# Value products of an expert layer with the table as the moving operand, and ten halves of gathered rows moved between stages

## The reference

```
q = (xb @ w_q).reshape(T, 8, 2, 128)                 # 8 heads, two halves
sc = einsum('thcd,hckd->thck', q, sub_keys)          # 128 keys per half
...                                                  # top 16 of 16x16 sums per head: idx, best
g = softmax(best)
act = gelu(einsum('td,thkd->thk', xb, u_tab[idx]))   # u_tab: 16384 x 2048
out = einsum('thkd,thk->td', v_tab[idx], g * act)    # v_tab: 16384 x 2048
x = x + out;  y = rmsnorm(x, final_norm_g)
```

## Time and profile before

| | |
|---|---|
| Median of three runs | 1714.14 us (1712.58 to 1718.35) |
| The profiled execution | 1717.41 us |
| Its span | 1715.6 us |
| TensorE busy with products | 1689.2 us, 98% |
| VectorE busy | 1455.6 us, 85% |
| ScalarE busy | 982.2 us, 57% |
| GpSimd busy | 475.9 us, 28% |
| Moved by DMA | 495.08 MB, mean 289 GB/s |
| Granted clock of TensorE | 0.997 of full speed, 2.4 GHz |

### The profile page before, as it was taken

The page is one execution under the profiler, slowest core; times in us unless marked ns, Lnnn a source line. Parts: engine busy times, 40 slices in busy tenths (PEclk is TensorE's granted clock), DMA queues, the critical chain, the costliest instruction groups (busy, mean ns, idle before and its releaser), DMA issues. The chain is left out here.

```text
span 1715.6 us, 28790 instructions
## 1 busy us (share of the span) xinstructions
PE 1689.2 (98%) x10886; PEld 1600.7 (93%) x10886; DVE 1455.6 (85%) x2068; ACT 982.2 (57%) x1589; POOL 475.9 (28%) x331
## 2 busy tenths in 40 slices
PE   8999999999999999999999999999999999999997
PEld 7887778878999999999999999999999999999997
DVE  4545777568799998999999999779999989999996
ACT  5555565453465557777766555555555555555554
POOL 0002310015320001111113354114454535444451
PEclk9999999999999999999999999999999999999999
DMA  6765455676677878888888999999999999999994
GB/s 230 217 185 169 148 159 159 192 253 198 195 232 230 268 234 295 284 274 281 269 278 306 399 399 403 310 271 393 381 390 384 377 327 362 383 390 384 376 378 180
DMA packets 135735, 495.08 MB, mean 289 GB/s; under 512 B 15424, under 2 KB 15456, under 8 KB 135088
## 3 DMA queue, kind: packets, MB, share of 16 engines
q1 hardware_dynamic: 95760, 347.65, 59.3%
q0 software_dynamic: 39552, 145.07, 23.2%
q10 hardware_dynamic: 288, 0.55, 0.1%
HBM read 487.86 MB, written 5.34 MB: 287 GB/s over the span
## 5 line engine op out<-in xcount | busy, mean ns | idle before, releaser
L750 ACT ACTIVATE HI<-V_RAW 128x1024 fp32r<-128x1024 f32 x256 | 271.9, 1062 | 258.0 <-PE PS L1711 123.3
L1671 PE MATMUL PS<-xT,HI 128*128 128x384 f32 x2048 | 414.1, 343 | 2.0 <-ACT HI L750 1.1
L1711 PE MATMUL PS<-W,HI 128*128 128x384 f32 x2048 | 411.0, 340 | 1.1 <-DVE OUTA L1330 0.6
L1671 PEld LDWEIGHTS PS<-xT,HI 128*128 128x128 f32 x2048 | 347.4, 188 | 9.8 <-ACT HI L750 7.5
L1711 PEld LDWEIGHTS PS<-W,HI 128*128 128x128 f32 x2048 | 347.8, 189 | 3.3 <-DVE OUTA L1330 1.9
L1219 DVE TENSOR_TENSOR V_LO<-V_RAW,HI 128x2048 fp32r<-128x2048 f32 x128 | 293.2, 2290 | 44.5 <-ACT HI L750 44.5
L750 ACT ACTIVATE HI<-RING_RAW 128x1024 fp32r<-128x1024 f32 x256 | 269.9, 1054 | 101.4 <-DMA RING_RAW<-u_t 95.6
L1226 DVE TENSOR_TENSOR RING_LO<-RING_RAW,HI 128x1024 fp32r<-128x1024 f32 x249 | 294.9, 1221 | 5.2 <-ACT HI L750 5.1
L526 POOL DMA_INDIRECT PICKED<-peer_u,PK x128 | 160.9, 1257 | 497.9 <-DVE DOTS L1278 420.6
L526 POOL DMA_INDIRECT PICKED<-peer_v,PK x128 | 212.3, 1659 | 242.7 <-DVE ACC L1283 217.4
L1716 PEld LDWEIGHTS PS<-W,V_LO 128*128 128x128 f32 x2048 | 265.7, 191 | 0.0
(11 more groups left out here) (218 smaller groups left out, 1586.8 us busy)
## 6 DMA issues: line engine op xcount, KB each, us to landing
RING_RAW<-u_t SPq DMA_DIRECT2D x256, 512.0 KB, 5.0
V_RAW<-peer_v SPq DMA_DIRECT2D x256, 512.0 KB, 9.3
RAW<-w_in SPq DMA_DIRECT2D x80, 512.0 KB, 3.8
RAW<-w_out SPq DMA_DIRECT2D x32, 512.0 KB, 3.9
RAW<-wq_t SPq DMA_DIRECT2D x32, 512.0 KB, 4.7
x_spill<-X POOLq DMA_DIRECT2D x2, 1024.0 KB, 5.8
PICKED<-peer_u,PK POOLq DMA_INDIRECT x128, 8.1
PICKED<-peer_v,PK POOLq DMA_INDIRECT x128, 9.1
```

Source lines behind the costliest of these rows:

```text
L750: nc.scalar.activation(HI[:, n % HI_SLOTS, :], raw_of(n), ACT.Copy).then_inc(top_ready, 1)
L1671: return mm(PS[:, j % S_BANKS, 0:2 * ND].rearrange("p (a t) -> p a t", a=2), HI[:, n % HI_SLOTS, kk * P:(kk + 1) * P], xT[:, k, :, 0:ND], ...
L1711: return mm(PS[:, V_BANKS[i], 0:2 * ND].rearrange("p (a t) -> p a t", a=2), HI[:, v % HI_SLOTS, i * P:(i + 1) * P], weights_of(v), start=v ...
```

## The change

The value product is turned. The gated scores are now the stationary operand, 128 tokens at a time, and the table moves, 512 columns at a time. The 192 tokens' high and low parts, 384 columns of `W`, are laid out as three blocks of 128: tokens 0 to 127 high; tokens 128 to 191 high with their low beside; tokens 0 to 127 low. The results lie with tokens on partitions, in banks A (tokens 0 to 127) and B (tokens 128 to 191, high on partitions 0 to 63 and low on 64 to 127). There is one pass over the 128 steps, a step's two halves one after the other, so eight banks hold all 2048 columns. The ring has 12 slots. Weights are made once per four units (before, per two). At the end no transposes are needed: VectorE adds the banks to the residual, ScalarE copies the lower half of B over to `OTHER`, and GpSimd adds the gathered rows to the residual.

Of the gathered halves 92 stand in scoring, not 102: every fifth step of those from 36 to 86 has none. The value stage has 164, not 154, spread over units 14 to 241 with no gap in the middle.

```
-V_RING = 10
-V_PLACE = [8, 9, 4, 5, 6, 7, 0, 1, 2, 3]
+V_RING = 12
+V_PLACE = [10, 11, 6, 7, 8, 9, 2, 3, 4, 5, 0, 1]
...
-HALF_STEPS = sorted(list(range(SPREAD0 - 3, NKEYS - 7)) + list(range(SPREAD_END, NKEYS - 7, 2)))
-FREE_UNITS = [u for u in range(14, 250) if not NKEYS - 6 <= u < NKEYS + 2]
+HALF_STEPS = sorted([j for j in range(SPREAD0 - 3, SPREAD_END) if j % 5] + list(range(SPREAD_END, NKEYS - 7))
+                    + list(range(SPREAD_END, NKEYS - 7, 2)))
+FREE_UNITS = range(14, 242)
...
-V_BANKS = (5, 6, 7, 3, 4, 2, 0, 1)
+BANK_A, BANK_B = (5, 6, 4, 2), (7, 3, 0, 1)
...
         def weights_of(v):
-            return WHL[v // 2 % W_PAIRS][:, v % 2]
+            return WHL[v // 4 % W_PAIRS][:, v // 2 % 2]
...
+                if v == V_RING - 2:
+                    sp.wait_ge(summed, NKEYS)
...
-                    half, j = divmod(v, NKEYS)
+                    j, half = divmod(v, 2)
                     src = v_view[:, j, half * UNIT:(half + 1) * UNIT]
...  (GpSimd, after the last gather)
+            for half in range(2):
+                cols = slice(half * HALF, (half + 1) * HALF)
+                nc.gpsimd.tensor_tensor(X1R[NS:P, 1, cols], X1R[NS:P, 1, cols], ACC4[NS:P, cols], ALU.add)
+            for half in range(2):
+                cols = slice(half * HALF, (half + 1) * HALF)
+                nc.gpsimd.tensor_tensor(X1R[NS:P, 1, cols], X1R[NS:P, 1, cols], OTHER[NS:P, cols], ALU.add)
...  (VectorE, weights_lo)
+                for dst, first, end in ((ND, P, ND), (2 * ND - P, 0, P)):
+                    ins = v.tensor_tensor(pair[:, :, dst:dst + end - first], store[:, j:j + 2, first:end],
+                                          pair[:, :, first:end].bitcast(FP32), ALU.subtract)
...  (VectorE, add_out of 512 columns c)
+                v.tensor_tensor(X1R[0:NS, 1, cols], PS[0:NS, BANK_B[c], :], X1R[0:NS, 1, cols], ALU.add)
+                v.tensor_tensor(X1R[:, 0, cols], PS[:, BANK_A[c], :], X1R[:, 0, cols], ALU.add)
+                v.tensor_tensor(X1R[0:NS, 1, cols], OTHER[0:NS, cols], X1R[0:NS, 1, cols], ALU.add)
...  (TensorE)
-            def value_high(v, i):
-                return mm(PS[:, V_BANKS[i], 0:2 * ND].rearrange("p (a t) -> p a t", a=2),
-                          HI[:, v % HI_SLOTS, i * P:(i + 1) * P], weights_of(v),
-                          start=v % NKEYS == 0, stop=False)
-            def value_low(v, i):
-                return mm(PS[:, V_BANKS[i], 0:ND], low_of(N_U + v)[:, i * P:(i + 1) * P],
-                          weights_of(v)[:, 0, :], start=False, stop=v % NKEYS == NKEYS - 1)
+            def value_high(v, c):
+                cols, w, b = HI[:, v % HI_SLOTS, c * BANK:(c + 1) * BANK], weights_of(v), 2 * (v % 2) + c
+                mm(PS[:, BANK_B[b], :], w[:, P:2 * ND - P], cols, start=v < 2, stop=False)
+                mm(PS[:, BANK_A[b], :], w[:, 0:P], cols, start=v < 2, stop=False)
+                return mm(PS[:, BANK_A[b], :], w[:, 2 * ND - P:2 * ND], cols, start=False, stop=False)
+            def value_low(v, c, last=False):
+                cols, w, b = low_of(N_U + v)[:, c * BANK:(c + 1) * BANK], weights_of(v), 2 * (v % 2) + c
+                low_b = mm(PS[:, BANK_B[b], :], w[:, P:2 * ND - P], cols, start=False, stop=last)
+                low_a = mm(PS[:, BANK_A[b], :], w[:, 0:P], cols, start=False, stop=last)
+                return low_b, low_a
```

More of the change, by code:

```diff
@@ L862, in final_scale @@
                     .then_inc(act_scaled, 1)
+            low_out_of(0)
+            low_out_of(1)
             act.wait_ge(fg_ready, 16 * D // BANK)
-            final_squares(0, 0)
-            final_squares(0, 1)
-            root(8, SS[:, 6:7])
-            final_squares(1, 0)
-            for c, col in ((2, 3), (3, 10)):
-                act.wait_ge(out_added, 4 + c + 1)
-                squares(X1R[:, 1, c * BANK:(c + 1) * BANK], col, FJ[:, 0:BANK])
+            final_squares(0, slice(0, HALF), 3, 0)
+            low_out_of(2)
+            act.wait_ge(rows_in, 4)
+            final_squares(1, slice(0, HALF), 4, 1)
+            low_out_of(3)
+            for c, cols in ((2, slice(HALF, HALF + BANK)), (3, slice(HALF + BANK, D))):
+                for tt in range(TT):
+                    final_squares(tt, cols, 2 * c + tt + 1, (2 + tt) if c == 2 else (10 + tt))
+                    if c == 3 and tt == 0:
+                        root(8, SS[:, 6:7])
             final_scale(0, slice(0, BANK))
@@ L1324, in _ @@
                     weights_lo(0)
-            def flush(half, i, dst):
-                dve.wait_ge(half_done, DT * half + i + 1)
-                v.tensor_reduce(dst[:, i, 0:ND], PS[:, V_BANKS[i], 0:2 * ND].rearrange("p (a t) -> p t a", a=2), AX.X, ALU.add)\
-                    .then_inc(flushed, 1)
             for u in range(N_V):
+                if u % 4 == 2 and u + 6 < N_V:
+                    weights_lo(u // 4 + 2)
                 if u % 2 == 0:
-                    if u + 4 < N_V:
-                        weights_lo(u // 2 + 2)
-                    if u == NKEYS - 2:
-                        for i in range(DT):
-                            flush(0, i, OUTA)
                     low_pair(u + 4)
-                if u == 0:
-                    dve.wait_ge(ones, N_BATCH)
-                    v.tensor_reduce(SEL4[:], IDENT[:].rearrange("p (s t) -> p t s", t=NS), AX.X, ALU.add).then_inc(sel_ready, 1)
                 if u in HALF_UNITS:
@@ new lines, in value_lows, with value_done @@
+                ins.then_inc(low_used, 1)
+            def value_done(v, c):
+                low_b, low_a = value_low(v, c, True)
+                low_b.then_inc(b_done, 1)
+                low_a.then_inc(a_done, 1)
+            for v in range(N_V - 1):
+                pe.wait_ge(top_ready, N_U + v + 1)
+                if v % 4 == 0:
+                    pe.wait_ge(w_lo, v // 4 + 1)
+                for c in range(2):
+                    if v == 1:
+                        pe.wait_ge(summed, NKEYS - 1 + c)
+                    ins = value_high(v, c)
+                ins.then_inc(top_used, 1)
+                if v:
+                    value_lows(v - 1)
@@ L1781 @@
+            low_wait(N_U + N_V - 2)
+            for c in range(2):
+                value_done(N_V - 2, c)
+            pe.wait_ge(top_ready, N_U + N_V)
+            low_wait(N_U + N_V - 1)
+            for c in range(2):
+                value_high(N_V - 1, c)
+                value_done(N_V - 1, c)
 def kernel(**inputs):
```

175 lines of the change are left out of this document (68 added, 107 removed).

## The result

The changed kernel takes 1704.42 us (median of 4 runs, 1703.03 to 1705.69); the kernel before, beside it, 1715.28 (4 runs, 1712.58 to 1718.35). The ratio is 0.9936, 95% interval [0.9919, 0.9953]: about 11 us, 0.6% faster. 1697 was forecast, with 1687 to 1710 as the range.

The account below looks back on a forecast made before the run. TensorE was taken to bound the value stage and VectorE scoring with gates, DMA near full. 1717.41 - 8.5 - 10.2 + 2 - 1.0 = 1699.7 us against the profile, as a median 1697 us; range 1687 to 1710.

Parts of the forecast that it names:

- the term of scoring: Scoring with gates: ten halves fewer free VectorE, -8.5 us, bounds 0 and -9.5.
- that of the value stage: Value stage: 584.0 us instead of 594.2, -10.2 us, bounds -13.5 and -5; 2 us added for short stalls.
- The 0.24 us more per pair, 9.5 us in all, is VectorE: its own step is 5.78 us: Scoring: pairs with a spread take 5.72 us instead of 5.48 because VectorE's own work sets them.
- the price of another wait: Rival in scoring: the 0.24 us per pair is not VectorE's, so 8.5 us stay; 1705 us, chance 0.08.
- VectorE's step is as long as TensorE's: Scoring: the argument given against the rival that scoring gives nothing back.
- The value unit: Value stage: ten 512-column products at 0.228 us make 2.28 us per unit; the turn itself gains 0.01 us per unit.
- The columns-alone rival: Value stage: turned products reach 0.216 us, TensorE needs 553 us, then the queue decides; down to 1690 us, chance 0.05.
- DMA stalls: Value stage: 2 us added for short stalls, bounds 0 and +14.
- the lag of 9 us: Value stage: DMA needs 2.32 us per unit, lagging 0.04 us over 228 units; the ring's 13 us slack covers it.
- 395 GB/s: Value stage: the DMA rate that new units ask for, (1 + 0.719) loads per 2.28 us, against 383 before.
- The dearer-loads rival: Value stage: successive loads of two halves of the same rows cost more; at 10% more 1731 us, chance 0.09.
- The end: Last value product to last scaling: 9.8 us instead of 10.8, -1.0 us, bounds -3 and +3.

Follow-up runs that it names:

- moved92: Changed kernel with ScalarE's scaling of the one-hot tables moved to the next step, behind the copy `HOLES` and the first `top`: 1695.91 us, ratio 0.9891.
- before92: Kernel before, value products not turned, with 92 gathered halves in scoring and 164 in the value stage: 1714.36 us, ratio 0.9999.
- before_moved: Kernel before with only ScalarE's scaling of the one-hot tables moved later in its program, 102 halves in scoring: 1705.99 us, ratio 0.9948.
- t102: Changed kernel with turned value products but 102 halves in scoring, as in the kernel before: 1704.91 us, ratio 0.9941.
- nohalf_spread: Changed kernel with no half in the 48 steps with a spread, 54 in scoring and 202 in the value stage: 1733.0 us, one run.
- loadorder: Changed kernel with value loads in the order of before, all left halves then all right ones: 1703.08 us, ratio 0.9937.
- pool_late: Changed kernel with GpSimd's two multiplications by the final gain waiting for all of VectorE's additions: 1707.88 us, one run.

## Why the prediction came out as it did

The direction, the range and the likeliest stage were right. The time was 7 us too low, and that it was not further off is luck: the term of scoring was too good by 8 us, and that of the value stage too poor by 5.5.

**Scoring: wrong, and the step that failed is "The 0.24 us more per pair, 9.5 us in all, is VectorE: its own step is 5.78 us".** The step was as long as the pair because VectorE was carried along by it. Two numbers that I had read spoke against it. The 1.46 us from a half to the next instruction hold 0.23 us of idle, marked "issue", before `TMP`; an engine that sets the pace has none, and in moved92 the same instruction follows at once. In 236 us of scoring it was busy 222.97, 94%, so 13 us, 0.3 per pair, were free, more than the excess to be explained. The right case was among the rivals ("the price of another wait"), with 1705 us and a chance of 0.08; what I wrote against it, "VectorE's step is as long as TensorE's", holds for every engine in a ring and tells nothing. The measured price of the ring is 9.1 us (moved92 against the changed kernel's 272.14), so the size of the excess was right and its owner wrong.

**The value unit: mechanism right, size at the lower bound.** 2.267 us, 10 x 0.2267. A product with new weights each time stands as far from the next as those in the earlier trace rows. The stage is 580.48, not 584.0 us. From the kernel before, 256 x (2.293 - 2.267) is 6.7 us, the pass change 2.75 (9.63 less three units) and the last unit 4.6 (6.9 less 2.29): 14.0 against 13.7 measured. The pass change is dearer in that one profile than elsewhere: in before92 and before_moved the same three units take 7.75 and 7.78 us, and the stages are 592.13 and 592.14 us. So the usual gain of the stage is 11.7 us, of which 6.7 are the turned unit and 5 what it lets fall. I had put the turned unit at 0.01 us, "almost nothing"; it is 0.026, times 256. The columns-alone rival (0.216 us) is false. The section that the prediction names for it in the Trainium skill (TensorE: Matmul & The Clock Gate, section Back-to-back issue gap) gives that formula for an isolated product, and about 131 ns for products of 512 columns in a sustained stream. The trace agrees with neither: it shows 226.7 ns.

**DMA stalls: +2 forecast, none measured.** What was wrong is the lag of 9 us, worked out as work over share, with 1.43 us of engine time for a load and a share of 1.02 as the most. But that time isn't a fixed price: in the same window of 1170 to 1380 it is 1.34 us in the changed kernel (59.2% of 210 us for 48.60 MB), where it was 1.45 before, and in that window the rate was 382 GB/s at a share of 1.02 in before, and 389, 393 and 398 GB/s at 1.01 in t102, before92 and the changed kernel, about what each asked for. Only nohalf_spread, at 409 GB/s, made TensorE wait. The forecast's own "395 GB/s" was right as a demand and not a limit.

**The dearer-loads rival: false.** Loads of the two halves of the same rows cost 1.34 us of engine time from 1170 to 1380, those of loadorder, in the old order, 1.36 (60.5% of 210 us for 48.99 MB), and loadorder's time is the same. The pitch within a load is the same in all runs, so none tests what it costs.

**The end: -1.0 forecast, +1.7 measured.** I had 12 additions at 0.65 us, to +5.1 after the last product. They start at -2.8, and ten of them take 0.60 from start to start, but two wait for GpSimd, which the forecast left out, so they end at +6.4. Last scaling at 11.4 where 9.8 was forecast. Another 1.1 us lies behind it: 4.7 us from the last scaling to the end of the span before, 5.74 to 5.81 in every turned kernel. The stores (2.1 MB) begin when the first block is scaled and run on at about 390 GB/s. The first is issued at 1708.51, 2.4 us ahead of the end of the last scaling, in the kernel before, and at 1694.02, 1.9 us ahead, now, which is half of the difference; where the other half comes from is not tested.

The sum of the profiled differences, -0.5 - 1.4 - 13.7 + 1.7 = -13.9 us, was forecast as -17.7. The missed 8.0 us of scoring were made good in part by the stage, 5.5 us with the stalls.

Two sums of the prediction are slightly off, and neither moves its time: 14.6 us over 48 steps are 0.30 us each, not 0.29, and the bound of -13.5 us for the stage belongs to 0.2267 us per product; 0.227 gives -12.8.

## What to carry to other kernels

When an engine's step is as long as the period, look for idle time in it, however short and however it is labelled, before calling it the bound: without any, the engine sets the pace; with some, follow the releases around until they close, and look for an instruction in one engine's program that stands ahead of the one the ring needs. Here moving it cost nothing, and taking work off that stood beside the ring, 10 or 48 halves, gave nothing. Here a DMA share of 1.01 to 1.02 went with anything from 382 to 398 GB/s, so it didn't show that the engines could do no more; ask which engine waits for a load, and what the rate is when it does.

## What the runs showed of the hardware that was not expected

- **A neighbour on GpSimd lengthens some of VectorE's instructions.** A 64 x 512 addition with both inputs in SBUF takes 0.67 us, and 1.62 when it starts under one of GpSimd's multiplications; additions with one input in PSUM take 0.67 in the same microseconds (1688.09). In pool_late two SCALAR_TENSOR_TENSOR of 128 x 1 elements went from 0.16 to 1.80 and 2.26 us, while a TENSOR_SCALAR of that size kept its 0.15 (1691.83). The Trainium skill (SBUF — State Buffer, section SBUF: two separate sides) says that a VectorE instruction with two SBUF inputs and a GpSimd instruction that reads SBUF share a port pair, and that the one that starts first holds it for its whole instruction. The trace agrees: only instructions with two SBUF inputs are slowed, and not by a factor. They end with or just behind the GpSimd instruction that they meet: in the changed kernel the multiplications end at 1687.61 and 1690.37, the slow additions at 1688.16 and 1690.91; in pool_late the multiplications end at 1693.80 and 1696.10, the slow instructions at 1693.82 and 1696.11. An addition that started 0.25 us before the first multiplication (1684.71) took its 0.67.
- **Engine time per load was lower where more was moved**: 1.45 us per 512 KB load in the kernel before (63.7% of 210 us, 48.30 MB), 1.38 in before92, with the same order and ring, and 1.34 in the changed one; gathers took 1.30 in before and 1.32 in the changed one. The highest mean over 240 us on this one core was 409 GB/s.
- **512-column products with new weights each time stand 0.2267 us apart**, 2560 in a row over 580 us, at a granted clock of 1.00 in this stage (2.4 GHz), as far as products of two with the same weights in the projections.
